# Two transformer blocks in split fp32 on one NeuronCore: layer loops written out, weight rings without skips, and the low halves of the weights moved from GpSimd to VectorE

## What is computed

```
block 1, per layer:
  proj = rmsnorm(x) @ w_in            # gating, state-space, attention and gate columns
  y_a  = spatial gating; y_b = Mamba2 scan; y_c = differential attention
  x   += (g0*(y_a@w_branch_a) + g1*(y_b@w_branch_b) + g2*(y_c@w_branch_c)) @ w_out
  up   = causal_dwconv(rmsnorm(x) @ ffn_w_up); gate, val = split(up)
  x   += (silu(gate) * val) @ ffn_w_down
block 2, per layer:
  u, q, k, v, g_pool, g_attn = split(rmsnorm(h) @ w_in)
  h   += (sigmoid(g_pool)*(pool(u)@w_a) + sigmoid(g_attn)*(dilated_attention(q,k,v)@w_b)) @ w_o
  a, g = split(rmsnorm(h) @ w_up);  h += (gelu(dwconv(a)) * g) @ w_down
out = rmsnorm(h, norm_f)
```

## Time and profile before

| | us |
|---|---|
| median of three runs | 1999.43 |
| the profiled execution, its own time | 2002.12 |
| its span | 2000.3 |
| TensorE busy | 1918.8 |
| VectorE busy | 1061.0 |
| ScalarE busy | 1044.5 |
| GpSimd busy | 1182.1 |

### The profile page before, as it was taken

How to read it: one execution, slowest core, us unless ns; L and a number is a source line. 1 busy time by engine, 2 the same in 40 slices (tenths; PEclk the granted TensorE clock), 3 DMA queues, 4 the chain that set the end, 5 groups by cost and what they waited for, 6 DMA issues and landing times.

```text
span 2000.3 us, 36536 instructions
## 1 busy us (share of the span) xinstructions
PE 1918.8 (96%) x14342; PEld 1835.4 (92%) x14342; DVE 1061.0 (53%) x1421; ACT 1044.5 (52%) x1172; POOL 1182.1 (59%) x1094
## 2 busy tenths in 40 slices
PE   5999999999899999999999999999999999999998
PEld 5999998998799999899989999989988999989997
DVE  4657556765275655676634144455544233356553
ACT  5556634655364754465534356455444446455443
POOL 3555556766455655757755656456765565466665
PEclk9999999999999999999999999999999999999999
DMA  8887745555565563655664477455555557455554
GB/s 181 154 152 138 138 159 183 177 192 191 149 142 142 145 152 128 201 170 167 203 201 150 146 196 190 144 195 183 170 187 175 162 174 198 112 200 169 167 174 147
DMA packets 298971, 335.13 MB, mean 168 GB/s; under 512 B 8169, under 2 KB 266485, under 8 KB 298785
## 3 DMA queue, kind: packets, MB, share of 16 engines
q1 hardware_dynamic: 298664, 332.53, 58.6%
q10 hardware_dynamic: 120, 0.09, 0.0%
HBM read 331.52 MB, written 1.07 MB: 166 GB/s over the span
## 4 chain that ended last, share of the span: by engine, by line
POOL 53%; issue 39%; PE 6%; POOLq 0%; ACT 0%; DMA 0%; DVE 0%; DVEq 0%; SPq 0%; ACTq 0%
POOL w_low L350 53%; PE proj_ps L533 3%; PE proj_ps L544 1%; PE proj_ps L543 1%; PE proj_ps L545 1%; POOLq L348 0%; DMA x<-in_x 0%; ACT tmp L875 0%; PE chain_ps L600 0%; DVE x L1791 0%; ACT w_hi L361 0%; ACT L885 0%; ACT act_hi L885 0%; DVE x L1623 0%; DVEq L136 0%
## 5 line engine op out<-in xcount | busy, mean ns | idle before, releaser
L350 POOL TENSOR_TENSOR w_low<-w_raw,w_hi 128x256 fp32r<-128x256 f32 (+1 forms) x1088 | 1181.6, 1115 | 810.7 <-ACT w_hi L361 810.7
L533 PE MATMUL proj_ps<-act_hi,w_hi 128*128 128x256 f32 x3296 | 953.1, 289 | 49.8 <-POOL w_low L350 33.6
L533 PE MATMUL proj_ps<-act_lo,w_hi 128*128 128x256 f32 x3296 | 941.1, 286 | 0.0
L533 PE MATMUL proj_ps<-act_hi,w_low 128*128 128x256 f32 x3296 | 940.8, 285 | 0.0
L361 ACT ACTIVATE w_hi<-w_raw 128x2048 fp32r<-128x2048 f32 (+3 forms) x326 | 584.3, 1794 | 249.9 <-PE proj_ps L545 147.2
L533 PEld LDWEIGHTS proj_ps<-act_hi,w_hi 128*128 128x128 f32 x3296 | 640.7, 194 | 61.9 <-issue 49.3
L350 DVE TENSOR_TENSOR w_low<-w_raw,w_hi 128x1024 fp32r<-128x1024 f32 (+2 forms) x326 | 429.7, 1319 | 474.4 <-ACT w_hi L361 470.2
L533 PEld LDWEIGHTS proj_ps<-act_lo,w_hi 128*128 128x128 f32 x3296 | 641.0, 194 | 0.5
L533 PEld LDWEIGHTS proj_ps<-act_hi,w_low 128*128 128x128 f32 x3296 | 640.5, 194 | 0.0
L543 PE MATMUL proj_ps<-w_hi,act_hi 128*128 128x512 f32 x480 | 187.5, 391 | 0.0
L544 PE MATMUL proj_ps<-w_low,act_hi 128*128 128x512 f32 x480 | 186.9, 389 | 0.0
(11 more groups left out here) (219 smaller groups left out, 1418.9 us busy)
## 6 DMA issues: line engine op xcount, KB each, us to landing
w_raw<-in_w_in SPq DMA_DIRECT2D x126, 1024.0 KB, 7.7
w_raw<-in_ffn_w_up SPq DMA_DIRECT2D x44, 1024.0 KB, 5.2
w_raw<-in_w_up SPq DMA_DIRECT2D x44, 1024.0 KB, 5.1
w_raw<-in_ffn_w_down SPq DMA_DIRECT2D x16, 1024.0 KB, 5.1
w_raw<-in_w_down SPq DMA_DIRECT2D x16, 1024.0 KB, 5.0
w_raw<-in_w_branch_b SPq DMA_DIRECT2D x8, 1024.0 KB, 5.1
w_raw<-in_w_out SPq DMA_DIRECT2D x8, 1024.0 KB, 5.0
w_raw<-in_w_a SPq DMA_DIRECT2D x8, 1024.0 KB, 6.2
```

What stands on the lines that cost most here:

```text
L350: last = eng.tensor_tensor(group_view(wlo, slot, g)[:, part, :], group_view(raw, slot, g)[:, part, :], group_view(whi, HIGH_AT[b][n], g)[: ...
L533: last = mm(o, held, moved, start=start and k == ks[0] and q == 0, stop=stop and k == ks[-1] and q == 2, skip_group_check=shared)
```

## The change

1. The hardware loops over the layers are gone: `for i in range(LAYERS)` writes both passes out on every engine, and all semaphore values are constants.
2. The rings run on through all 326 groups: group q takes slot q % 5 and q % 3. `ring`, the skips, `SPLITS` and the two loads past the end (`AHEAD`) are gone. Every conversion waits for group q - 3, every load for group q - 5.
3. Four conversions per pair of passes (XBC2, UP2 in block 1; PU2, UP2 in block 2) are `LATE`: ScalarE does them right behind the root, VectorE behind the first two normed pairs. For XBC2 and PU2 that was their place before; UP2's was behind OUT3.
4. VectorE makes both halves of each low part, in two instructions with a semaphore each; TensorE waits for `w_lo_front` at the group's start and for `w_lo_back` at the k-tile where the second half begins. GpSimd has nothing to do.
5. `norm` sums the squares behind the low parts of pairs 2 and 3 instead of ahead of them, with two `tensor_scalar` instructions in place of one `tensor_tensor`.

```diff
-        def low_part(eng, b, i, n, G, on_pool):
-            cut = g["kt"] - POOL_K[g["kt"]]
-            ks = slice(cut, g["kt"]) if on_pool else slice(0, cut)
-            eng.wait_ge(w_hi, plain_count(b, i, n + 1))
-            for part in ([slice(k, k + 1) for k in range(cut, g["kt"])] if on_pool else [ks]):
-                last = eng.tensor_tensor(...)
-            last.then_inc(w_lo_pool if on_pool else w_lo_dve, 1)
+        FRONT = {8: 4, 4: 2, 3: 2, 2: 1}
+        def low_part(dve, q):
+            cut = FRONT[g["kt"]]
+            dve.wait_ge(w_hi, q + 1)
+            dve.tensor_tensor(lo[:, 0:cut, :], of[:, 0:cut, :], hi[:, 0:cut, :], ALU.subtract).then_inc(w_lo_front, 1)
+            dve.tensor_tensor(lo[:, cut:, :], of[:, cut:, :], hi[:, cut:, :], ALU.subtract).then_inc(w_lo_back, 1)
...
-            act.wait_ge(group_done, count(b, i, HIGH_LAST[b][n] + 1))
+            act.wait_ge(group_done, q - HIGH + 1 + LOW)
...
-                pe.wait_ge(w_lo_dve, plain_count(b, i, n + 1))
-                pe.wait_ge(w_lo_pool, plain_count(b, i, n + 1))
+                pe.wait_ge(w_lo_front, plain_count(b, i, n + 1))
...
                 for k in ks:
+                    if t == 0 and k == FRONT[g["kt"]]:
+                        pe.wait_ge(w_lo_back, q + 1)
...
-            with pe.Fori(0, LAYERS) as i:
+            for i in range(LAYERS):
...
-            def norm(b, i, which, a0, G=None):
-                mean_square(b, i, which)
+            def norm(b, i, which, a0, late):
                 xg_low(b, i, which, 2)
                 xg_low(b, i, which, 3)
+                mean_square(b, i, which)
                 norm_rstd(layer(b, i) * 2 + (which + 1))
                 normed(b, which, 0)
                 normed(b, which, 1)
-                if G is not None:
-                    split_behind(b, i, -1, G)
+                low_part(V, at_group(b, i, at_name[b][late]))
```

More of the change, by code:

```diff
@@ L28 @@
 DN_K = (4, 4, 4, 4, 3, 3)
[L31 to L43, removed]
 def build_program(nc, t_in, out):
@@ L247, in build_program, with at_group, splits @@
         at_name = {b: {g["name"]: n for n, g in enumerate(G)} for b, G in ((1, G1), (2, G2))}
[L248 to L262, removed]
+        GROUPS = [(b, i, n, g) for b, G in ((1, G1), (2, G2)) for i in range(LAYERS) for n, g in enumerate(G)]
+        def at_group(b, i, n):
+            return BASE[b] + i * NG[b] + n
+        LATE = [at_group(b, i, at_name[b][name]) for b, names in ((1, ("XBC2", "UP2")), (2, ("PU2", "UP2"))) for i in range(LAYERS) for name in names]
+        def splits(b, i, n):
+            q = at_group(b, i, n) + HIGH
+            return [q] if q < len(GROUPS) and q not in LATE else []
         def half_count(b, i, which, c):
@@ L586, in proj_two @@
                         for t in range(2):
-                            last = products(G[q], q, t, range(2 * p, 2 * p + 2), p == 0 and t == 0, p == PAIRS - 1 and t == 1, a0, True)
+                            last = products(G[q], at_group(b, i, q), t, range(2 * p, 2 * p + 2), p == 0 and t == 0, p == PAIRS - 1 and t == 1, a0, True)
                         if p == PAIRS - 1:
@@ L956, in _ @@
             x_squares(1, 0, 0, 1)
-            for n in range(AHEAD):
-                high_part(act, 1, 0, n, G1)
-            with act.Fori(0, LAYERS) as i:
+            for q in range(2):
+                high_part(act, q)
+            for i in range(LAYERS):
                 xg_high(1, i, 0, 2)
@@ L1281, in mean_square @@
                 dve.wait_ge(step("sq"), half_count(b, i, which, 1) + 1)
-                TTo(rstd[:, :], ssq[:, 0:2], ssq[:, 2:4], ALU.add).then_inc(step("ms"), 1)
-            def norm(b, i, which, a0, G=None):
-                mean_square(b, i, which)
+                for tt in range(TT):
+                    last = V.tensor_scalar(rstd[:, tt:tt + 1], ssq[:, tt:tt + 1], ssq[:, 2 + tt:3 + tt], None, ALU.add)
+                last.then_inc(step("ms"), 1)
+            def norm(b, i, which, a0, late):
                 xg_low(b, i, which, 2)
                 xg_low(b, i, which, 3)
+                mean_square(b, i, which)
                 norm_rstd(layer(b, i) * 2 + (which + 1))
@@ L1352, in _ @@
             TTo(bias_row[:, 0:511], pC[0:12, 510::-1], qkv[0:12, 1024:1535][:, ::-1], ALU.add).then_inc(step("bias_row"), 1)
-            for n in range(AHEAD):
-                low_part(V, 1, 0, n, G1, False)
-            with dve.Fori(0, LAYERS) as i:
-                norm(1, i, 0, A_H, G1)
+            for q in range(2):
+                low_part(V, q)
+            for i in range(LAYERS):
+                norm(1, i, 0, A_H, "XBC2")
                 def dt_abs():
@@ L1702, in _ @@
                         up_stream(1, i, n, g, G1)
-            with dve.Fori(0, LAYERS) as i:
+            for i in range(LAYERS):
                 dve.wait_ge(step("par_in2"), i * 32 + 32)
-                norm(2, i, 0, A_H, G2)
+                norm(2, i, 0, A_H, "PU2")
                 def b2_max(u):
```

100 lines of the change are left out of this document (44 added, 56 removed).

## The result

The changed kernel takes 1975.43 us (median of four runs, 1974.82 to 1975.54), the kernel before 1999.25 beside it: a ratio of 0.9878, 95% interval 0.9861 to 0.9896, 24 us less. The profiled executions stand at 1975.42 and 2002.12, 26.7 apart; the sum of the forecast, 28.9, was made against the latter.

A forecast was written before the change was run, and what follows sets the result against it. TensorE, busy 1918.8 of 2000.3 us, was taken as the bound. Terms 1.0 + 29.8 + 2.2 + 7.8 - 5.6 - 3.4 - 2.9 = 28.9 us off 2002.1 gave 1973.2, median 1970.5; 8-in-10 range 1954 to 1988.

The forecast's parts named there:

- D: Block 1's branch between passes: the refill after the jump goes, XBC3 starts earlier; gain 7.8 us.
- A: Kernel start: VectorE brings the first and second groups 2.6 us earlier, XBC3 then waits for its bank; net gain 1.0 us.
- B: Groups behind skips and short groups, plus WA3 and UP12: TensorE's waits for GpSimd's low parts go; gain 29.8 us.
- C: PU in block 2: PU3's wait of 1.33 us goes, PU2's low part stands ahead of a bank; gain 2.2 us.
- E: UP0 to UP3: VectorE's longer chain delays UP3's bank, 2.1 us twice in block 1, 0.7 twice in block 2; sum -5.6.
- G: TensorE's clock: lower-level stretches behind WA3 and UP12 go, +3.0 us; new gaps at UP3 and XBC3 cost 5.9; net -2.9.
- F: Steps behind two VectorE halves: block 2's softmax loses 2.4 us, the opening of the scan 1.0; sum -3.4.
- VectorE's busy time: Whole kernel: forecast to go from 1061 to about 1340 us (68%), 294 more halves at 1.1, 50 less by contention gone.
- VectorE late in more places: Rival: second halves also delay scan, attention and middle stage, 12 to 17 us go; about 1985 us; chance 0.17.
- The clock staying up at the new gaps: Rival: clock stays up at the new gaps and TensorE meets its banks, 10 us better; 1960 us; chance 0.13.
- The branch stall in straight-line code: Rival: written-out code stalls at fetch too, so the branch's gain is gone; 1979 us; chance 0.05.
- VectorE the bound of block 1: Rival: a UP pair costs VectorE 13.0 us against 12.0 today, +22 us over 22 pairs; about 2004 us; chance 0.05.

The follow-up runs named there:

- the square of four kernels: Changed kernel and three variants of it: second half on GpSimd or VectorE, wait at start or middle; GpSimd 1985.2 and 1962.2 us, VectorE 1975.1 and 1975.4.

## Why the prediction was right, and where not

The time (1975.4 for 1970.5), the direction and the range held. Against its own execution the sum said 28.9, and the profiled executions lie 26.7 apart. That the total came so close is in part luck: D gave 7 us less than forecast, block 2 gave 7 more, and one line of the diff had no term.

**A, the start:** 1.0, as forecast.

**B, the waits for GpSimd:** the size was right (9.2 and 11.9 forecast in block 1, 10.6 and 11.8 measured, 1.5 of the former being a shorter stretch at the lower clock at GA0, which differs from trace to trace), the reason was not. The step said that the back half is there "1.14 us later, while TensorE needs 2.9 us to reach it. That is 2.6 us earlier than GpSimd's last piece, more than any of these waits". Both halves of that reasoning remove the wait behind short groups on their own, and I credited the first. GpSimd's last piece, at 3.8 to 4.3, was early enough for the middle of a group: the square of four kernels and the one moved wait show it. And the 11.9 behind the skips are won by the rings alone, with GpSimd and the wait at the start. The sum should have been made with each part of the change by itself, above all with the wait moved and GpSimd kept.

**C, PU:** 1.2 instead of 2.2; the sum of squares took the rest.

**D, the branch:** 7.8 forecast, 0.6 measured. The failed step is "XBC0 at about 533.0 (its bank is late by 1.8 by VectorE's residual)". The bank was 6.1 late, and XBC3 started 31.4 us behind the last DN matmul, not 26 (33.5 before). The standstill at the branch did go, as the loops alone show, but the residual was behind the low part of XBC1, and that behind a load. I had priced the chain with the loads' times of before: XBC1's took 9.1 us from issue to landing, and takes 13.9 in the changed kernel (below). The reading of the earlier trace rows that "issue" is the branch back, twice, was wrong as well: the wait of 3.1 is at XBC1 in the start, and the 3.44 went away in the kernel with the moved wait while its loop stayed. What the branch shows in both kernels with loops is VectorE standing still for 11 to 12 us.

**E, UP0:** the mechanism (the first conv, late behind more halves) is there, mis-sized. Forecast were 2.1 in block 1 and 0.7 in block 2. Measured is a wait of 1.8 at UP3 in both, since block 2 has the same conv in front, which the step denied; and at UP2's second scaled pair another 0.41 with its restart, which no term had. With the clock it is 3.4 a norm, 13.6, where E and the new part of G had 11.5.

**Part 5 of the change** had no term at all. Its order costs 0.7 to 0.8 at each of six norms, 4.4 us in the traces and 5.4 by the run's median, nearly as much as E.

**F** did not happen: block 2 won 15.6 where B, the clock and F made 8.3. TensorE goes from Q0 to WB0 in 205.0 us where it took 205.3, so the halves ahead of the softmax delayed nothing. Another 2.4 of the difference are the waits of UP4 and UP5, which E had counted.

**G, the clock:** it fell behind all four gaps of 1.8 at UP3, 1.5 us each, and not directly behind those of 2.9 at XBC3. Gaps of 0.69 and 0.94 at UP3 left it up, but so did three of four gaps of 1.8 in the kernel with the sum of squares ahead, so no length of gap can be given.

**VectorE's busy time** is 1282.2, not about 1340. The second halves took 367.1 us, where the sum had some 320, but with GpSimd silent the rest fell by some 145 us, where it had 50.

**The rivals.** VectorE late in more places: no. The clock staying up at the new gaps: no, it fell at all four UP3. The branch stall in straight-line code: no; no "issue" wait of a fetch inside a pass. VectorE the bound of block 1: no; a pair of UP takes 11.5 us, halves follow each other at 1.14 (347.65 and 348.79 above), and VectorE waits 0.8 us at each gate half. The figure of "VectorE: DVE Perf Modes" in the Trainium skill (where the cycles go), elements plus about 150 cycles, fits one instruction alone (1.22 us), but two in a row overlap by 0.08, so the traces decide against 2.45 for a pair: it takes 2.36, which is 0.09 less and not 0.1 to 0.15.

## What to carry to other kernels

When an engine waits at a group's start for two producers, ask first when it needs each, and move the wait there: that cost one wait and gave more here than moving the work, which had to be paid for in the chains behind a norm that ran through the new engine. On an engine with a fixed program, look at each step that another engine waits for and ask whether what stands ahead of it is needed by it; a residual behind an unrelated low part and a sum of squares behind four low parts cost some 6 and 5 us. A forecast needs a term for every line of the diff, the small reordering too.

## What was not expected of the hardware

With the compute engines' loops written out, loads became slower, though SyncE, which issues them, runs the same written-out program in both. The issues of `w_in` in the page's part 6, first of the kernel before, then of the same kernel with nothing but those loops written out (KB each, median us from issue to landing):

```profile
w_raw<-in_w_in SPq DMA_DIRECT2D x126, 1024.0 KB, 7.7
```

```profile
w_raw<-in_w_in SPq DMA_DIRECT2D x126, 1024.0 KB, 8.7
```

These medians mix two blocks. Block 2's loads of `w_in` have a median of 5.1 to 5.3 in every kernel. Block 1's have 9.8 in the kernel before, 9.5 in the other kernel with hardware loops (the one with the moved wait), and 12.0 to 13.1 in the twelve with the loops written out. The packets are as many and as large (1 KB each, pieces of rows of about 32 KB in block 1). In the changed kernel there are stretches in which the DMA engines are full and move little; from 515 to 520, ahead of the late XBC1, against 480 to 490:

```profile
480.00:490.00 10.00, 10.00 (x46) 8.29 (x45) 4.19 (x4) 3.88 (x3) 0.00 (x0) 1.00 0.68 210
515.00:520.00 5.00, 5.00 (x23) 4.13 (x23) 2.30 (x2) 1.92 (x1) 0.00 (x0) 1.00 1.02 86
```

86 GB/s at full share. Such stretches are in the trace of before too, fewer and milder. It is not the loads' own program, which has constant addresses in both. Why the other engines' written-out programs should do this stays open; no run was made for it.
